# A hybrid attention and PEER layer in three spans of tiles: spans regrouped to 1, 4 and 4 tiles, ranking one group ahead, expert steps during the score stage

## The reference, cut to what matters

```
def blk(tb):
    q = jnp.einsum("td,de->te", tb, wq).reshape(-1, PEER_HEADS, 2, PEER_HALF)
    sc = jnp.einsum("thjd,hjnd->thjn", q, subkeys).astype(jnp.float32)
    s1, i1 = lax.top_k(sc[:, :, 0], PEER_TOPK)
    s2, i2 = lax.top_k(sc[:, :, 1], PEER_TOPK)
    ...
    best, sel = lax.top_k(cand, PEER_TOPK)
    idx = jnp.take_along_axis(cidx, sel, axis=-1)
    g = jax.nn.softmax(best, axis=-1).astype(tb.dtype)
    ue = jnp.take(u, idx, axis=0)
    ve = jnp.take(v, idx, axis=0)
    a = jax.nn.gelu(jnp.einsum("thkd,td->thk", ue, tb), approximate=False)
    return jnp.einsum("thk,thkd->td", g * a, ve)
```

## The kernel before, in words

| stage | span 0 | span 1 | span 2 |
|---|---|---|---|
| inputs | 0 | 31 to 62 | 213 to 281 |
| attend | 0 | 63 to 133 | 282 to 458 |
| merge | 0 | 135 to 174 | 461 to 528 |
| out | 0 | 178 to 185 | 533 to 549 |
| score | 0 to 29 | 186 to 209 | 552 to 594 |

## Time and profile before

### The profile page before, as it was taken

The page is one execution under the profiler, slowest core; times in us unless marked ns, Lnnn a source line. Parts: engine busy times, 40 slices in busy tenths (PEclk is TensorE's granted clock), DMA queues, the critical chain, the costliest instruction groups (busy, mean ns, idle before and its releaser), DMA issues.

```text
span 4450.6 us, 39027 instructions
## 1 busy us (share of the span) xinstructions
PE 2849.2 (64%) x12071; PEld 1499.1 (34%) x12071; DVE 2446.5 (55%) x6358; ACT 795.1 (18%) x1696; POOL 2346.7 (53%) x2128
## 2 busy tenths in 40 slices
PE   7779668777897878677777799783233233233334
PEld 5468546434453434443434344341000000000000
DVE  1241454677344456387788455566665666666651
ACT  1230012333111112133333111111000000000000
POOL 0000224344343346376666564567777777777774
PEclk9769889777998989877777899896555555656556
DMA  7244668777977979899999998899999999999998
GB/s 243 89 140 137 227 233 309 252 257 263 330 274 267 341 274 397 284 331 355 339 337 330 362 373 322 319 376 363 363 375 366 379 371 378 368 370 364 371 367 284
DMA packets 552141, 1388.83 MB, mean 312 GB/s; under 512 B 51296, under 2 KB 253024, under 8 KB 551936
## 3 DMA queue, kind: packets, MB, share of 16 engines
q0 software_dynamic: 304128, 1107.43, 67.0%
q1 hardware_dynamic: 227408, 249.27, 17.1%
q10 hardware_dynamic: 20400, 29.64, 2.0%
HBM read 1326.10 MB, written 60.05 MB: 311 GB/s over the span
## 4 chain that ended last, share of the span: by engine, by line
PE 34%; POOL 23%; issue 13%; DVE 12%; DMA 10%; ACT 4%; DVEq 2%; another core or an unknown queue 1%; SPq 1%; ACTq 0%; POOLq 0%
POOL G_v_rows L569 12%; POOL G_u_rows L569 11%; PE scores L695 8%; PE scores L1452 8%; PE y_sum L1942 4%; PE scores L1456 4%; PE scores L1641 3%; DVE G_u_rows L1778 3%; DMA G_v_rows<-in_peer_v,G_idxT 2%; PE scores L1538 2%; DMA DF_w_br<-scratch_skT 2%; ACT C_probs L1260 2%; DVE C_probs L1327 1%; PE o L1209 1%; DVE C_probs L1351 1%
## 5 line engine op out<-in xcount | busy, mean ns | idle before, releaser
L569 POOL DMA_INDIRECT G_v_rows<-in_peer_v,G_idxT x1056 | 1180.9, 1118 | 1066.6 <-PE y_sum L1942 720.9
L1778 DVE CUSTOM_DVE_ANT_0 G_u_rows<-G_u_rows,G_h 128x1024 f32<-128x1024 f32 x1056 | 1276.3, 1221 | 529.5 <-DMA G_u_rows<-in_peer_u,G_idx 482.5
L569 POOL DMA_INDIRECT G_u_rows<-in_peer_u,G_idx x1056 | 1161.6, 1100 | 726.7 <-issue 314.4
L1942 PE MATMUL y_sum<-G_v_rows,G_zw 128*32 128x512 f32 x4224 | 792.5, 888 | 1000.9 <-DMA G_v_rows<-in_peer_v,G_idxT 961.8
L1942 PEld LDWEIGHTS y_sum<-G_v_rows,G_zw 128*32 128x32 f32 x4224 | 155.7, 142 | 1531.5 <-issue 1526.2
L1452 PE MATMUL scores<-D_hT,D_w_gate 128*128 128x256 f32 (+2 forms) x768 | 238.2, 464 | 0.0
L695 PE MATMUL scores<-A_w_in,A_hT 128*128 128x256 f32 (+2 forms) x864 | 223.5, 420 | 9.7 <-ACT A_hT L783 5.6
L695 PEld LDWEIGHTS scores<-A_w_in,A_hT 128*128 128x128 f32 x864 | 171.1, 200 | 63.3 <-issue 14.3
L1192 PE MATMUL turn<-ident,C_probs 128*128 128x128 f32 (+1 forms) x647 | 142.1, 337 | 72.1 <-ACT C_pT L1272 52.5
L1452 PEld LDWEIGHTS scores<-D_hT,D_w_gate 128*128 128x128 f32 x768 | 145.2, 191 | 92.7 <-issue 54.2
L548 POOL MEMSET G_zw<- 128x1024 f32 x2 | 1.8, 956 | 292.8 <-SPq L521 292.8
(11 more groups left out here) (282 smaller groups left out, 3822.0 us busy)
## 6 DMA issues: line engine op xcount, KB each, us to landing
A_w_in<-in_w_in SPq DMA_DIRECT2D x24, 1024.0 KB
D_w_gate<-in_w_gate SPq DMA_DIRECT2D x24, 1024.0 KB
G_u_rows<-in_peer_u,G_idx POOLq DMA_INDIRECT x1056
G_v_rows<-in_peer_v,G_idxT POOLq DMA_INDIRECT x1056
DF_w<-in_w_gate SPq DMA_DIRECT2D x12, 1024.0 KB
DF_w<-in_peer_wq SPq DMA_DIRECT2D x12, 1024.0 KB
F_w_q<-in_peer_wq SPq DMA_DIRECT2D x12, 1024.0 KB
G_sc<-scratch_sc ACTq DMA_DIRECT2D x66, 128.0 KB
```

The lines of the kernel that those rows point to most:

```text
L569: pool.indirect_dma_start(out=buf[:, :], out_offset=None, in_=table, in_offset=bass.IndirectOffsetOnAxis(ap=rows, axis=0)).then_inc(signal ...
L1778: dve.tensor_tensor_reduce(out=self.u_rows[slot][:, :], in0=self.u_rows[slot][:, :], in1=self.h2[t % 2][:, :], scale=1.0, scalar=0.0, op0= ...
L1942: last = pe.matmul(self.ps_y[32 * c:32 * (c + 1), cols], self.zw[b % 2][:, at:at + 32], self.v_rows[(4 * quad + c) % SLOTS_G][:, cols], st ...
```

## The change

1. **Spans.** `RUNS` sets the spans to tile 0; tiles 1, 2, 3 and the sample; tiles 4 to 7. Their columns are 128, 416 and 512. The expert groups follow in that order (`ORDER`, `GROUP`, `FIRST`: tile 1 begins at group 8, the sample at group 32, tile 4 at group 34). Scratch columns of queries, hT and oT are laid out by place in this order, keys and outputs by tile number.
2. **Ranking.** `AHEAD` goes from 2 to 1: a group is ranked during the one ahead of it, in its steps 0, 2, 4 and 6, with the gate in step 8.
3. **Plan.** Everything but score is to stand at least 24 steps ahead of the step where the span's first tile is due, and the score stage is spread from there over 88 steps, head by head, with the expert steps of the tile before and of the new tile between its ticks.
4. **Out stage.** The buffers `E_xt` are gone: the residual rows are loaded straight into `E_x1`, and for the third and fourth tile SyncE waits until the stores of two tiles ago have landed. Where the span has more than 416 columns (span 2), the first three chunks of w_o are no longer loaded during merge.
5. `load_h2` and `load_x1` stand at steps counted from the tile's first group.

The new plan, in the same form:

| stage | span 0 | span 1 | span 2 |
|---|---|---|---|
| inputs | 0 | 22 to 41 | 196 to 255 |
| attend | 0 | 42 to 78 | 256 to 426 |
| merge | 0 | 78 to 98 | 429 to 501 |
| out | 0 | 100 to 105 | 506 to 521 |
| score | 0 to 21 | 105 to 193 | 521 to 609 |

The planner's attend costs are now 76.7, 384.4 and 610.2.

```diff
+RUNS = ((0,), (1, 2, 3, SAMPLE), (4, 5, 6, 7))
+SPANS = [Span(i, run, sum(len(r) for r in RUNS[:i])) for i, run in enumerate(RUNS)]
+ORDER = [t for run in RUNS for t in run]
...
-AHEAD = 2
+AHEAD = 1
+GOAL = 24 + 4 * TOPK
...
-            end = 2 + P * sp.tiles[0] - (AHEAD + 1) * TOPK
-            total, sofar = sum(cost for _, cost in own), 0.0
-            for _, cost in own:
+            first = AHEAD + TOPK * FIRST[sp.place] - 24
+            goal = 2 * HEADS + 5 if sp.i == 0 else first + GOAL
+            scoring = sum(cost for name, cost in own if name == "score")
+            dense = sum(cost for _, cost in own) - scoring
+            turn = min(first, done + int((goal - done) * dense / (dense + scoring))) if sp.i else 0
+            sofar, heads = 0.0, 0
+            for name, cost in own:
                 sofar += cost
-                out.append(done + int((end - done) * sofar / total))
-            done = end
+                if name != "score":
+                    out.append(done + int((turn - done) * sofar / dense))
+                    continue
+                heads += 1
+                steps = turn + int((goal - turn) * (sofar - dense) / scoring)
+                out.append(max(0, min(steps, first + TOPK * max(0, heads // 2 - 1))))
+            done = out[-1]
...
-                if g == 0 and b == BRANCHES - 1:
+                if g == 0 and b == BRANCHES - 1 and sp.n <= W_O_EARLY:
                     self.load_w_o(eng, self.E[i], range(W_O_HEAD))
...
             if t >= 2:
-                eng.wait_ge(self.e_added, self.nt0[i] + t - 1)
+                eng.wait_ge(self.e_out[t % 2], self.e_out0[t % 2][i] + 32 * (t // 2))
             r = sp.rows[t]
-            eng.dma_start(m["xt"][t % 2][0:r, :], a["x_all"][sp.lo + t * P:sp.lo + t * P + r, :]).then_inc(self.e_x[t % 2], 16)
+            eng.dma_start(m["x1"][t % 2][0:r, :], a["x_all"][sp.tiles[t] * P:sp.tiles[t] * P + r, :]).then_inc(self.e_x[t % 2], 16)
...
-                if c in (3, 6, 9, 12):
-                    self.rank(dve, m, c // 3 - 1)
-                if c == 15:
+                if c in (0, 2, 4, 6):
+                    self.rank(dve, m, c // 2)
+                if c == 8:
                     self.gate(dve, m)
```

More of the change, by code:

```diff
@@ L58, with __init__, own @@
 class Span:
[L61 to L67, removed]
-        self.cols = slice(self.lo, self.lo + self.width)
-SPANS = [Span(i, lo, hi) for i, (lo, hi) in enumerate(((0, 2), (2, 5), (5, TILES)))]
+    def __init__(self, i, tiles, place):
+        self.i, self.tiles, self.nt, self.place = i, list(tiles), len(tiles), place
+        self.sample = SAMPLE in tiles
+        self.prompt = self.nt - self.sample
+        self.rows = [min(P, TOK - t * P) for t in tiles]
+        self.lo, self.n, self.width = place * P, sum(self.rows), self.nt * P
+        self.keys = (max(t for t in tiles if t < SAMPLE) + 1) * P
+        self.cols = slice(self.lo, self.lo + self.width)
+    def own(self, k):
+        return slice(self.tiles[k] * P, (self.tiles[k] + 1) * P)
+RUNS = ((0,), (1, 2, 3, SAMPLE), (4, 5, 6, 7))
+SPANS = [Span(i, run, sum(len(r) for r in RUNS[:i])) for i, run in enumerate(RUNS)]
+ORDER = [t for run in RUNS for t in run]
 STAGES = [(sp.i, name) for sp in SPANS for name in ("inputs", "memory", "attend", "merge", "out", "score")
@@ L187, with tile_end @@
 STEPS = U_SLOTS + V_LAG + 4
-AHEAD = 2
+AHEAD = 1
+GOAL = 24 + 4 * TOPK
 QUADS = BLOCK // 4
+GROUP = [(at, t, h) for at, t in enumerate(ORDER) for h in range(2 if t == SAMPLE else HEADS)]
+FIRST = [next(n for n, g in enumerate(GROUP) if g[0] == at) for at in range(TILES)] + [GROUPS_ALL]
+H2_LOADED = [sum(64 if t == SAMPLE else 16 for t in ORDER[at % 2:at + 1:2]) for at in range(TILES)]
+PIECES = [sum(64 if t == SAMPLE else 256 for t in ORDER[:at]) for at in range(TILES + 1)]
 def span_of(t):
     return next(sp for sp in SPANS if t in sp.tiles)
-def tile_end(t):
-    return (min(4 * t + 3, 32) + 1) * BLOCK - 1 + V_LAG if t < SAMPLE else U_SLOTS - 1 + V_LAG
+def tile_end(at):
+    return FIRST[at + 1] * TOPK - 1 + V_LAG
 class Kernel:
@@ L501, in weave @@
             done += 1
-        assert done == STEPS + 2, done
+        assert done == STEPS + AHEAD, done
     def dense(self, inputs, memory, attend, merge, out, score, eng):
@@ L1409, in attend_dve @@
         take_o(len(jobs) - 1)
+        if o.last["diff"] + 2 == o.n:
+            norm_o(PAIRS - 1)
         dve.drain().then_inc(self.dve_left, 1)
@@ L1507, in store @@
             r = sp.rows[t]
-            own = slice(sp.lo + t * P, sp.lo + t * P + r)
+            own = slice(sp.tiles[t] * P, sp.tiles[t] * P + r)
             eng.dma_start(s["x1"][own, :], m["x1"][t % 2][0:r, :]).then_inc(self.e_out[t % 2], 16)
@@ L1521, in out_sp @@
         self.load_score(eng, sp, 0)
-        for k in range(2):
+        for k in range(min(2, nt)):
             eng.wait_ge(self.e_out[k], self.e_out0[k][i] + 32 * ((nt + 1 - k) // 2))
@@ L1601, in score_sp @@
         self.open_stage(eng, i, "score")
-        prompt = nt - sp.sample
+        prompt = sp.prompt
         scores = 2 * nt // 2
@@ L1617, in score_sp @@
             yield
-        if not sp.sample:
+        if i + 1 < len(SPANS):
             self.first_inputs(eng, SPANS[i + 1])
@@ L1768, in experts_dve @@
             yield
-        finish = {tile_end(t) + 2: t for t in range(TILES)}
+        finish = {tile_end(at) + 2: at for at in range(TILES)}
         for k in range(STEPS):
@@ L1856, in store_y @@
-    def store_y(self, act, t):
-        act.wait_ge(self.y_ready, t + 1)
-        for at, row in self.rows_of(t):
-            lo = P + t * P + row
-            act.dma_start(self.s["y"][lo:lo + 8, :], self.x1[at:at + 8, :]).then_inc(self.y_out, 16)
+        if at:
+            act.wait_ge(self.y_out, PIECES[at])
+        for lo, row in self.rows_of(t):
+            act.dma_start(self.x1[lo:lo + 8, :], self.s["x1"][t * P + row:t * P + row + 8, :]).then_inc(self.x1_in, 16)
+    def store_y(self, act, at):
+        act.wait_ge(self.y_ready, at + 1)
+        for lo, row in self.rows_of(ORDER[at]):
+            to = P + ORDER[at] * P + row
+            act.dma_start(self.s["y"][to:to + 8, :], self.x1[lo:lo + 8, :]).then_inc(self.y_out, 16)
@@ L1928, in weigh_rows @@
         b, i = divmod(quad, QUADS)
[L1929 removed]
+        at = GROUP[2 * b][0]
+        first, last_of = 2 * b == FIRST[at] and i == 0, 2 * b + 2 == FIRST[at + 1] and i == QUADS - 1
         if i == 0:
             pe.wait_ge(self.z_made, b + 1)
[L1932 to L1934 removed]
+        if first and at:
+            pe.wait_ge(self.y_taken, at)
         for c in range(4):
```

123 lines of the change are left out of this document (56 added, 67 removed).

## The result

The changed kernel takes 4641.81 us (median of 4 runs, 4629.26 to 4658.33) against 4452.94 (median of 4) for the kernel before: a ratio of 1.0424, 95% interval 1.0401 to 1.0447. The profiled execution's span is 4640.9 us. The prediction said 4650, in a range of 4540 to 4740. The change makes the kernel slower, as forecast.

A forecast was written before the change was run, and what follows sets the result against it. Dense work was taken to set the pace up to the tail, where DMA is the bound at 2.894 us a step. A dense part ending at 3259 us plus a 1390 us tail gave 4649, forecast as 4650 us, range 4540 to 4740.

The forecast's parts named there:

- The sum of 4649 us: Whole kernel: dense part ending at 3259 us plus a tail of 1390 us gives the forecast span.
- F = 22.5, a = 0.579, c = 1.64: Attend: fixed part 22.5 us, 0.579 per planner's cost unit, 1.64 us a step, fitted to three stages.
- 98: Span 0's merge: forecast 98 us, from 128-column products at 0.158 us and 8 us of first loading.
- 80: Span 0's score stage: forecast about 80 us, where it took 120.9 us for 27 steps before.
- 296 us each: Score stages of spans 1 and 2: 88 steps at 2.894 us plus 41 us of the stage's own transfer.
- Rival B: Span 1's attend: thinner steps lower TensorE's clock, 45 us more than the sum, 4695 us; chance 0.10.
- Rival C: Score stages: ranks come late, the chain per head uncovered, up to 180 us more, 4830 us; chance 0.12.
- The chain of 36 us against 23: Score during steps: tick, store and load of scores take 36 us a head, against 23 us of 8 steps.
- Rivals D and E: Under dense work: D, steps dearer than taken, 4500 to 4590 us, chance 0.13; E, DMA bound, 4380 us, chance 0.08.
- my mean of 1.2: Spans 1 and 2: mean cost taken for a step under dense work, 1.2 us, making the change cost 198 us.
- The break-even of 2.4: Under dense work: at 2.4 us a step, the 161 steps fewer there pay back the change's 198 us.
- The head start: Span 0: the first gather goes out near 390 us, where it went out at 514.1 us before.

The follow-up runs named there:

- Without steps: The kernel before, and the changed kernel, each with its expert steps left out (y not computed): spans of 2411.9 us (before) and 2423.2 us (changed).
- the run with 44 steps: The changed kernel with GOAL = 44 in place of 88, so about half as many steps in the score stages: ratio 1.0279 to the kernel before.
- ranking alone: The kernel before with only the ranking changed, one group ahead, the plan kept: 4414.43 us against 4420.23, ratio 0.999.
- the old spans and 44 steps: The changed kernel with spans set back to tiles 0-1, 2-4, 5-7 and the sample, and GOAL = 44: ratio 0.9861 to the kernel before.
- the sample in span 1: The changed kernel with GOAL = 44 and spans of tiles 0-1, 2-4 and the sample, 5-7: ratio 0.9824 to the kernel before.

## Why the prediction was right, and where it was not

**The bound.** That the dense work sets the pace up to the tail, that a step costs little there and 2.894 us (measured after: 1200/413 = 2.906) in the tail, and that the regrouping takes steps from the cheap part, came out as forecast. The sum of 4649 us stood against a span of 4640.9 (with the 1.8 and 0.8 us that the prediction adds it comes to 4652, not 4650). Its marks: span 1's score begins at 1281.5 us (forecast 1296), ends at 1592.7 (1592); the dense part ends at 3230.8 (3259); the tail takes 1410 (1390).

**That closeness is luck in part: it hides errors of both signs.** The stages of spans 1 and 2 miss by 26 us too much to 35 too little. The step "F = 22.5, a = 0.579, c = 1.64" failed: three stages for three unknowns left nothing to check the form with. Without steps attend takes 263 and 443 us where the fit gives 226 and 345, and a step costs 1.1 (1.48 in the changed span 1), not 1.64. For span 1's attend, with few steps, this was 35 us too little (304 against 339); for span 2's, with steps as before, 26 too much. "98" for span 0's merge was wrong by 27: 577 matmuls of 128 columns take 66.9 us of TensorE, 0.116 each and not the 0.158 of the short products in the score stage. "80" for span 0's score was 99: without steps it is 56, and 20 steps cost 43. The trace shows where 27 of the 43 go (start and duration in us, in brackets the idle time before):

```profile
366.04 0.31 ACT L1895 ACTIVATE G_egate<-G_best,G_nbest 128x16 f32<-128x16 f32 x1 [19.80 <-DVEq L1747]
366.34 0.42 ACT L1695 ACTIVATE F_qT<-scores 128x128 f32<-128x128 f32 x2
366.82 1.22 PE L1680 MATMUL scores<-F_skT,F_qT 128*128 128x128 f32 x4 [26.91 <-issue]
```

In ScalarE's stream the exponential for group 1's gate (G_egate) stands ahead of the copy of the next queries (F_qT). It waited 19.8 us for VectorE's ranking of group 1, which runs between the first dots, and TensorE, which needs the copy, stood still for 26.9. In the kernel before its longest wait for this copy was 13.4 us. Inputs of span 1 took 233, not 251, and the out stages 74 and 95, not 85 and 108: without steps the out stage takes 70 us for the last span in the old order of loads (a fourth tile of 32 rows) and 69 and 72 in the new, so the residual behind a landing store and the later w_o cost 2 us at most.

**The score stages.** 296 us each was the forecast; 311 and 294 were measured, with the DMA share at 0.93 and not 0.97 or more, and with TensorE waiting on v rows for 110 us in the first. The size was right, and the run with 44 steps shows that the number of steps makes it. DMA is less full than forecast at the start of the stage. There the matmuls of a whole head stand on TensorE ahead of the first y_sum, and GpSimd, its buffers full, issues no gather for 26.5 us:

```profile
1314.98 1.55 POOL L595 DMA_INDIRECT G_u_rows<-in_peer_u,G_idx  x1 [26.48 <-PE y_sum L1969]
```

Up to 1310 us the DMA share is 0.65, and 0.96 in the rest of the stage.

**Rival B, the clock.** Attend's clock fell from 0.72 to 0.61, as was feared, and the dense matmuls took about 36 us more of TensorE's time than at 0.72. The stage came out 35 us longer than the sum had it. That the fit of the rates is wrong and that the clock has a price are not told apart by these runs: B is neither shown nor out. What it was priced at, 45 us, is too much even if TensorE were the bound.

**Rival C, late ranks.** Nothing of it in spans 1 and 2: in the whole changed kernel VectorE waits once for loaded scores, 3.5 us, in span 0, and ranking alone is 0.999. The chain of 36 us against 23 was covered. Only at the start of the steps, in span 0's score, did a late rank cost time, the 27 us above.

**Rivals D and E, dearer steps.** Under dense work a step costs 0.93 to 1.06 us in both kernels, below my mean of 1.2. The break-even of 2.4 is far off.

**The head start** of 164 us is real and worth nothing here. Tile 0 alone gives 128 steps; the last span's first tile is due at step 544, where it was 640, and what counts is how many of the 1056 steps can stand under inputs to out: 500 in spans 1 and 2 before, 412 after, 553 with the old spans and 44 steps, 580 with the sample in span 1. The last two beat both kernels, by about 1.4% and 1.8% of the time before.

## What to carry to other kernels

Here one stream of work, the gathers, is bound by DMA's bandwidth and woven into compute. In such a case, run the compute without the stream, work out from it what a unit of the stream costs in each stage, and count the units at each price; an earlier start or a fuller stage says little by itself. A stage takes on the stream at the cheap price only until its transfers are as long as the stage. Past that point a further unit costs as much as it costs alone: 1.15 us a step for the first 44 in a score stage, 2.98 for the next 44, 2.91 in the tail. A fit with as many unknowns as rows is not a measurement, even if the sum comes out.

## What the runs showed of the hardware that was not expected

A 128x128 by 128-column float32 matmul instruction takes 66.9/577 = 0.116 us in a merge stage at a clock of 0.97, about half of the 126.81/577 = 0.22 of 256 columns. The weight loads beside it are busy for 66.35/577 = 0.115 each, just as long, and still the stage falls from 128.6 to 71.3 us. Some 160 added 256-column matmuls in an attend stage raised the granted clock from 0.60 to 0.85 and the time by 7 us. The gathers' steps do the same when there are enough: the same dense matmuls of span 1's attend took 186.4 us of TensorE at 0.72 beside 71 steps, and 221.8 at 0.61 alone.
